# Two transformer blocks on one core: the first two jobs take x without its norm, x arrives in column blocks, and ada blocks change places

## The reference

```python
def rmsnorm(x, g):
    xf = x.astype(jnp.float32)
    y = xf * lax.rsqrt(jnp.mean(jnp.square(xf), axis=-1, keepdims=True) + NORM_EPS)
    return (y * g.astype(jnp.float32)).astype(x.dtype)
...
        h = rmsnorm(x, g[0])
        proj = h @ w_in[l]
        (u_pool, u_conv, c_gate, b_gate_conv, q, k, v, qi, ki, wi) = jnp.split(proj, pts, axis=-1)
...
        dots = jnp.einsum('bthd,bsd->bths', qib.astype(jnp.float32), k_idx32)
        score = jnp.einsum('bth,bths->bts', wb.astype(jnp.float32) * IDX_HEADS ** -0.5,
                           jax.nn.relu(dots))
...
        shift, scale, gate = jnp.split(silu_c @ w_ada[l] + b_ada[l], 3, axis=-1)
```

## Time and profile before

| what | value |
|---|---|
| median of three runs | 2193.26 us (2193.22 to 2193.27) |
| the profiled execution's own time | 2193.32 us |
| its span, first to last instruction | 2191.5 us |
| mean granted TensorE clock | 0.999 |
| TensorE busy | 2180.9 us, 15930 products |
| VectorE busy | 1546.1 us, 71% |
| ScalarE busy | 1060.4 us, 48% |
| GpSimd busy | 103.1 us |
| DMA | 474.97 MB, mean 217 GB/s |

### The profile page before, as it was taken

How to read it: one execution, slowest core, us unless ns; L and a number is a source line. 1 busy time by engine, 2 the same in 40 slices (tenths; PEclk the granted TensorE clock), 3 DMA queues, 4 the chain that set the end, 5 groups by cost and what they waited for, 6 DMA issues and landing times.

```text
span 2191.5 us, 37576 instructions
## 1 busy us (share of the span) xinstructions
PE 2180.9 (100%) x15930; PEld 2050.2 (94%) x15930; DVE 1546.1 (71%) x1886; ACT 1060.4 (48%) x1382; POOL 103.1 (5%) x84
## 2 busy tenths in 40 slices
PE   9999999999999999999999999999999999999998
PEld 9999999999999889989988988998889999999987
DVE  7899588888889657544554555555768887776776
ACT  5444445544444546444543443444655555444443
POOL 1000000000000000000000000000101211110001
PEclk9999999999999999999999999999999999999999
DMA  8876676687787755656656656656755545678784
GB/s 276 245 242 199 199 252 223 227 279 259 253 282 263 240 183 182 194 192 193 195 194 194 194 194 196 200 191 204 246 172 164 165 136 178 220 269 285 257 276 158
DMA packets 248032, 474.97 MB, mean 217 GB/s; under 512 B 21526, under 2 KB 26000, under 8 KB 247096
## 3 DMA queue, kind: packets, MB, share of 16 engines
q1 hardware_dynamic: 243032, 454.40, 64.9%
q0 software_dynamic: 4832, 18.16, 2.5%
HBM read 468.30 MB, written 5.78 MB: 216 GB/s over the span
## 4 chain that ended last, share of the span: by engine, by line
PE 98%; DVE 1%; issue 0%; ACT 0%; DMA 0%; SPq 0%; DVEq 0%; POOLq 0%; POOL 0%; ACTq 0%
PE ps L907 21%; PE ps L909 20%; PE ps L908 20%; PE ps L900 11%; PE ps L901 11%; PE ps L902 11%; PE ps L825 1%; PE ps L703 0%; PE ps L748 0%; DMA raw<-in_w_in 0%; PE ps L735 0%; PE ps L814 0%; PE ps L813 0%; PE ps L815 0%; DVE wloW L1298 0%
## 5 line engine op out<-in xcount | busy, mean ns | idle before, releaser
L907 PE MATMUL ps<-op0h,whiW 128*128 128x256 f32 x3376 | 936.9, 278 | 1.4 <-DVE wloW L1298 1.2
L909 PE MATMUL ps<-op0h,wloW 128*128 128x256 f32 x3376 | 932.3, 276 | 0.0
L908 PE MATMUL ps<-op0l,whiW 128*128 128x256 f32 x3376 | 932.2, 276 | 0.0
L1298 DVE TENSOR_TENSOR wloW<-raw,whiW 128x1024 fp32r<-128x1024 f32 (+1 forms) x503 | 618.2, 1241 | 312.3 <-ACT whiW L954 310.3
L954 ACT ACTIVATE whiW<-raw 128x1024 fp32r<-128x1024 f32 (+1 forms) x504 | 529.7, 1059 | 574.6 <-PE ps L909 469.2
L907 PEld LDWEIGHTS ps<-op0h,whiW 128*128 128x128 f32 x3376 | 633.8, 188 | 4.0 <-DVE wloW L1298 2.1
L908 PEld LDWEIGHTS ps<-op0l,whiW 128*128 128x128 f32 x3376 | 633.9, 188 | 0.6
L909 PEld LDWEIGHTS ps<-op0h,wloW 128*128 128x128 f32 x3376 | 633.8, 188 | 0.0
L1298 DVE TENSOR_TENSOR wloT<-raw,whiT 128x1024 fp32r<-128x1024 f32 (+1 forms) x264 | 318.9, 1218 | 236.2 <-ACT whiT L954 235.0
L954 ACT ACTIVATE whiT<-raw 128x1024 fp32r<-128x1024 f32 (+1 forms) x264 | 273.9, 1048 | 286.2 <-PE ps L902 246.4
L900 PE MATMUL ps<-whiT,op1h 128*128 128x512 f32 x640 | 249.2, 389 | 0.0
(11 more groups left out here) (310 smaller groups left out, 2088.4 us busy)
## 6 DMA issues: line engine op xcount, KB each, us to landing
raw<-in_w_in SPq DMA_DIRECT2D x256, 512.0 KB, 4.3
raw<-in_w_up SPq DMA_DIRECT2D x128, 512.0 KB, 3.8
raw<-in_w_down SPq DMA_DIRECT2D x128, 512.0 KB, 4.0
raw<-in_w_ada SPq DMA_DIRECT2D x96, 512.0 KB, 4.5
raw<-in_w_gate SPq DMA_DIRECT2D x96, 512.0 KB, 5.0
raw<-in_w_out SPq DMA_DIRECT2D x64, 512.0 KB, 4.8
raw<-in_w_branch SPq DMA_DIRECT2D x48, 512.0 KB, 5.0
raw<-in_w_proj_a SPq DMA_DIRECT2D x24, 512.0 KB, 5.0
```

Source lines behind the costliest of these rows:

```text
L907: pe.matmul(o, wh, xh[:, ka, :], start=first and m % 2 == 0, stop=False, skip_group_check=True)
L908: pe.matmul(o, wh, xl[:, ka, :], start=False, stop=False, skip_group_check=True)
L909: mm = pe.matmul(o, wl, xh[:, ka, :], start=False, stop=last, skip_group_check=True)
L1298: v.tensor_tensor(wlo[job.mode][q % NSPL][:, :, 0:job.n], x, h.bitcast(F32), ALU.subtract).then_inc(s_lo, 1)
```

## The change

- x is issued by ScalarE's queue in four blocks of 512 columns (both halves of the tokens), the norm gains behind the first; SyncE's queue begins with ident and the weights, and the gate's vectors come behind raw buffer 3.
- The first operand is x turned and scaled by the gain alone: ScalarE writes it to x0t, VectorE splits it (split_x0: a copy that rounds, and a subtraction). qi0 and qi1 take it so. The missing factor rstd goes into wi, which is scaled by it in vw's epilogue.
- The row sums move to steps 8 and 9, rstd behind them; x0_diagonal puts rstd on the diagonal of two 128x128 tiles, and one product with a matrix of ones spreads it over all partitions (256 columns). For pairs p = 0 to 7, at steps 12, 13, 14, 16, 17, 18, 20, 21, VectorE multiplies x0t by it (x0_norm), ScalarE rounds (x0_high) and, in the next step, VectorE subtracts (x0_low). kk's chunk p waits for pair p.
- The warm-ups are 7, 2 and 2 in place of 12, 4, 1 and 1.
- The load of pw waits for the eighth pair; vectors_b gets a transpose of 48 columns, and its sigmoid moves from step 6 to 23.
- ada blocks 0 to 12 stood behind chunks 10, 13, 16, 19, 22 and 32 to 53 in threes; they now stand behind 32 to 53 in threes (blocks 0 to 7) and 64, 69, 74, 79, 84. The quarters of blocks 0 to 7 move with them, from steps 36 and 37 to 51 and 52.

```diff
-        for q in (list(range(of["qi1"].first + 2, of["vw"].first, 3)) + list(range(of["pool0"].first, NQ, 3)))[:13] + list(range(of["q0"].first + 2, NQ, 3))[:51]:
+        for q in (list(range(of["pool0"].first, of["cc0"].first, 3)) + list(range(of["cb0"].first, of["q0"].first, 5)))[:13] + list(range(of["q0"].first + 2, NQ, 3))[:51]:
...
-        side(act_at, 6, "vectors_b")
-        side(dve_at, 7, "vectors_b", 1)
+        side(act_at, 23, "vectors_b")
+        side(dve_at, 24, "vectors_b", 1)
+        for tt in range(2):
+            side(act_at, 8 + tt, "x0_square", tt)
+            side(dve_at, 8 + tt, "x0_var", tt)
+        side(dve_at, 10, "x0_diagonal")
+        side(pe_at, 11, "x0_spread")
+        side(dve_at, 11, "x0_spread")
+        for p, q in enumerate((12, 13, 14, 16, 17, 18, 20, 21)):
+            side(dve_at, q, "x0_norm", p)
+            side(act_at, q, "x0_high", p)
+            side(dve_at, q + 1, "x0_low", p)
...
-            for t in range(2):
-                sp.dma_start(x0[:, t, :], rows_of("x", t)).then_inc(s_x[t], 16)
             sp.dma_start(ident[:, :], a["k_ident"]).then_inc(s_ident, 16)
-            sp.dma_start(vst[0:64, :], a["norm_gains"].rearrange("l g (r c) -> (l g r) c", c=128)).then_inc(s_va, 16)
-            sp.dma_start(vst[64:112, :], a["b_gate"].rearrange("l g (r c) -> (l g r) c", c=128)).then_inc(s_va, 16)
...
-            rstd("x0", 0)
-            rstd("x0", 1)
...
+            rstd("x0", 0)
+            rstd("x0", 1)
+            pool.wait_ge(s_xnop, 8)
+            pool.dma_start(pw[:, :, :, :], a["pool_w"].rearrange("l g (c p) d -> p (l g) c d", p=128)).then_inc(s_pw, 16)
...
+                pe.wait_ge(s_x[u // 2], 16)
+                if u >= 3:
+                    pe.wait_ge(s_x0s, 2 if u < 5 else u - 2)
+                for j in range(2):
+                    turn_x0_part(2 * u + j, turned_x0(u, j))
...
+            def x0_spread():
+                pe.wait_ge(s_ones, 1)
+                pe.wait_ge(s_diag, 1)
+                pe.wait_ge(s_oper, 8)
+                pe.matmul(bank[6][:, 0:256], ones, diagonal, start=True, stop=True).then_inc(s_spread, 1)
...
+                elif job.name == "kk":
+                    pe.wait_ge(s_xnop, k // 2 + 1)
...
-            warm(12)
+            warm(7)
             pe.wait_ge(s_ident, 16)
-            pe.wait_ge(s_va, 32)
-            pe.transpose(bank[7][:, 0:112], vst[0:112, :], ident[0:112, 0:112]).then_inc(s_vst, 1)
-            warm(4)
+            pe.wait_ge(s_va, 16)
+            pe.transpose(bank[2][:, 0:64], vst[0:64, :], ident[0:64, 0:64]).then_inc(s_vst, 1)
             turn_x(0)
-            warm(1)
+            warm(2)
             turn_x(1)
-            warm(1)
+            warm(2)
...
+            columns_of_x(0)
+            act.dma_start(vst[0:64, :], a["norm_gains"].rearrange("l g (r c) -> (l g r) c", c=128)).then_inc(s_va, 16)
+            for j in range(1, 4):
+                columns_of_x(j)
...
+            def x0_high(p):
+                act.wait_ge(s_pe, of["qi1"].first + p + 1)
+                act.wait_ge(s_xn, p + 1)
+                act.activation(op0h[:, 2 * p:2 * p + 2, :], x0t[:, 2 * p:2 * p + 2, :], ACT.Copy).then_inc(s_xnhi, 1)
...
+            act.activation(col("table"), tmp[0][:, 0:2], ACT.Identity).then_inc(s_table, 1)
+            act.wait_ge(s_vat, 1)
+            turn_x0_part(0, 0).then_inc(s_x0s, 1)
+            high_first(0)
+            turn_x0_part(0, 1).then_inc(s_x0s, 1)
+            high_first(1)
+            for i in range(1, 3):
+                turn_x(i)
...
+            def split_x0(u, j, n):
+                k = slice(2 * u + j, 2 * u + j + n)
+                v.wait_ge(s_x0s, u + j + 1 if u == 0 else u + 2)
+                v.tensor_copy(op0h[:, k, :], x0t[:, k, :]).then_inc(s_x0hi, 1)
+                v.wait_ge(s_x0hi, u + j + 1 if u == 0 else u + 2)
+                return v.tensor_tensor(op0l[:, k, :], x0t[:, k, :], op0h[:, k, :].bitcast(F32), ALU.subtract)
...
+            def x0_diagonal():
+                v.wait_ge(s_rstd, 2)
+                for tt in range(2):
+                    op = v.tensor_scalar(diagonal[:, 128 * tt:128 * tt + 128], ident[:, :], norm_col("x0", tt)[1], None, ALU.mult)
+                op.then_inc(s_diag, 1)
+            def x0_spread():
+                v.wait_ge(s_spread, 1)
+                v.tensor_copy(spread, bank[6][:, 0:256]).then_inc(s_rb, 1)
+                v.wait_ge(s_rb, 1)
+            def x0_norm(p):
+                x = x0t[:, 2 * p:2 * p + 2, :]
+                v.tensor_tensor(x, x, spread.unsqueeze(1).broadcast_to([128, 2, 256]), ALU.mult).then_inc(s_xn, 1)
+            def x0_low(p):
+                k = slice(2 * p, 2 * p + 2)
+                v.wait_ge(s_xnhi, p + 1)
+                v.tensor_tensor(op0l[:, k, :], x0t[:, k, :], op0h[:, k, :].bitcast(F32), ALU.subtract).then_inc(s_xnop, 1)
...
-                    v.tensor_scalar(wi[:, tt, :], b[:, 256:272], 0.25, None, ALU.mult).then_inc(s_pair[job.pair], 1)
+                    v.tensor_scalar(wi[:, tt, :], b[:, 256:272], norm_col("x0", tt)[1], 0.25, ALU.mult, ALU.mult).then_inc(s_pair[job.pair], 1)
...
+            split_x0(0, 0, 1).then_inc(s_oper0, 1)
             low_first(0)
-            x0_norm(1, 256, 512)
-            low_x0(0, 0)
...
-            low_x0(0, 1)
-            low(1)
-            turn_x(1)
-            low(2)
-            turn_x(2)
-            x0_norm(0, 1024, 2048)
-            x0_norm(1, 1024, 2048)
+            for i in range(1, 3):
+                turn_x(i)
+                low(i)
```

More of the change, by code:

```diff
@@ L329, in program @@
         a5 = tmp[5]
+        spread, diagonal, ones = tmp[4][:, 0:256], tmp[4][:, 256:512], tmp[5][:, 128:256]
         gqk = sb("gqk", [128, 2, 128])
@@ L432, in program @@
         s_const = sem("pool_constants")
-        s_x = [sem(f"x_rows{i}") for i in range(2)]
-        s_va, s_vb, s_ident = sem("vectors_a"), sem("vectors_b"), sem("ident")
+        s_x = [sem(f"x_columns{i}") for i in range(4)]
+        s_va, s_vg, s_vb, s_ident = sem("vectors_a"), sem("gate_vectors"), sem("vectors_b"), sem("ident")
         s_vst, s_vat, s_vsu, s_vbt, s_csig, s_csil = sem("va_turned"), sem("vat"), sem("vb_turned"), sem("vbt"), sem("c_sigmoid"), sem("c_silu")
@@ L704, in turn_x @@
                 mm.then_inc(s_turn, 1)
+            def x0_spread():
[3 more added lines that the diff above has]
+                pe.matmul(bank[6][:, 0:256], ones, diagonal, start=True, stop=True).then_inc(s_spread, 1)
             def vectors_b():
+                pe.wait_ge(s_vg, 16)
+                pe.transpose(bank[3][:, 256:304], vst[64:112, :], ident[64:112, 64:112])
                 pe.wait_ge(s_vb, 128)
@@ L847, in fourier_d @@
                 mm.then_inc(s_fd, 1)
-            parts = {"turn_x": turn_x, "vectors_b": vectors_b, "bias_row": bias_row, "ada_fold": ada_fold, "index_dots": index_dots, "pool_weight": pool_weight,
+            parts = {"turn_x": turn_x, "x0_spread": x0_spread, "vectors_b": vectors_b, "bias_row": bias_row, "ada_fold": ada_fold, "index_dots": index_dots, "pool_weight": pool_weight,
                      "scores1": scores1, "turn1": turn1, "values1": values1, "turn_x": turn_x,
@@ L971, in x2_square, with turn_x0_part @@
                 square(X, macc[:, tt, :], "x2", tt)
+            def turn_x0_part(u, j):
+                kt = 2 * u + j
+                act.wait_ge(s_turn0, 2 * u + 2 if u else kt + 1)
+                return act.activation(x0t[:, kt, :], turned_x0(u, j), ACT.Identity, scale=vat[:, kt:kt + 1])
             def turn_x0(u):
-                for kt in (2 * u, 2 * u + 1):
-                    act.wait_ge(s_turn0, kt + 1)
-                    act.activation(op0h[:, kt, :], bank[4 + kt % 4][:, 0:256], ACT.Identity, scale=vat[:, kt:kt + 1]).then_inc(s_x0hi, 1)
+                turn_x0_part(u, 0)
+                turn_x0_part(u, 1).then_inc(s_x0s, 1)
             def turn_x(u):
@@ L1366, in turn_x, with x0_var @@
                 v.tensor_tensor(l, x, h.bitcast(F32), ALU.subtract).then_inc(s_oper, 1)
+            def x0_var(tt):
+                part, (ss, rs), x = col("x0_parts")[:, tt:tt + 1], norm_col("x0", tt), x0[:, tt, 1024:2048]
+                for j in (2, 3):
+                    v.wait_ge(s_x[j], 16)
+                v.tensor_tensor_reduce(junk0[:, 1024:2048], x, x, 1.0, D * EPS, ALU.mult, ALU.add, ss).then_inc(own.sem, own.up())
+                v.wait_ge(own.sem, own.n)
+                v.wait_ge(s_sumsq, tt + 1)
+                v.tensor_scalar(rs, part, ss, 1.0 / D, ALU.add, ALU.mult).then_inc(s_var, 1)
+            def x0_diagonal():
+                v.wait_ge(s_rstd, 2)
+                for tt in range(2):
+                    op = v.tensor_scalar(diagonal[:, 128 * tt:128 * tt + 128], ident[:, :], norm_col("x0", tt)[1], None, ALU.mult)
[11 more added lines that the diff above has]
+                v.tensor_tensor(op0l[:, k, :], x0t[:, k, :], op0h[:, k, :].bitcast(F32), ALU.subtract).then_inc(s_xnop, 1)
```

97 lines of the change are left out of this document (36 added, 61 removed).

## The result

| | before | after |
|---|---|---|
| median of the runs | 2193.27 us (6 runs, 2193.20 to 2193.96) | 2204.98 us (6 runs, 2204.53 to 2206.07) |
| ratio | 1 | 1.0053, 95% interval 1.0043 to 1.0064 |
| profiled execution: own time, span | 2193.32, 2191.5 us | 2205.14, 2203.3 us |
| busy TensorE, VectorE, ScalarE | 2180.9, 1546.1, 1060.4 us | 2182.9, 1555.6, 1061.8 us |

The change makes the kernel 11.7 us slower; 7.15 us was forecast. The direction held, the range did not: 2205.0 lies 0.5 us above its upper end, 2204.5.

The account below looks back on a forecast made before the run. TensorE was taken as the bound (98% of the span), so only its time without products could change: -4.2 + 0.3 + 0.75 + 5.3 + 5.0 = +7.15 on 2193.3 gives 2200.4 us, range 2196.5 to 2204.5.

Parts of the forecast that it names:

- the start, up to the end of chunk 0: Ahead of TensorE's first product: it comes at 8.9 us, after fewer warm-ups and smaller first loads; -4.2 us.
- chunks 1 and 2: Behind the first chunk: the weight split now follows the turn of the pair, 3.7 us against 3.6; +0.3 us.
- the 48-column transpose, chunk 5: TensorE's own new work: one transpose of 48 columns adds 0.05 us.
- the diagonal's product: TensorE's own new work: one float32 product of 256 columns spreading rstd over all partitions; 0.7 us.
- the norm during qi1 and kk: TensorE waits ahead of chunks 20 to 23 for VectorE and ScalarE to norm eight pairs; +5.3 us.
- the ada blocks and quarters: Ahead of low(70), VectorE has no gap for added blocks 8, 9 and two quarters; TensorE waits, +5.0 us.
- The data must be there by then: At the start: x and w's 1 MB, ident and gains land near 5.8 us, operands are ready at 8.5.
- rival of the late loads: At the start: loads on two queues share, first product near 12 us, about 2202.5 us in all; chance 0.05.
- The ping-pong: In qi1 and kk: VectorE and ScalarE alternate in order, 3.63 us per pair against TensorE's 2.04; +5.3 us.
- The clock: Rival: clock falls in TensorE's pauses ahead of chunks 20-23 and 65-70, costing 1.7 to 3.4 us; chance 0.15.

Follow-up runs that it names:

- e13: e8 with x, gains and weights all loaded on SyncE's queue in the order of need; 2191.51 us (10 runs), ratio to before 0.9991.
- e6: The changed kernel with four of GpSimd's loads (cm, gqk twice, recip) moved behind the store of the bias row; 2203.70 us.
- e7: The changed kernel with the gains' load ahead of x's first block and GpSimd's four loads later; 2203.15 us.
- e8: The changed kernel with five ada blocks and two quarters later, x0_norm one step earlier, gains first, GpSimd's four loads later; 2191.47 us, ratio to before 0.9992.
- e12: The kernel before with x loaded in four blocks of 512 columns instead of two token halves, still on SyncE's queue; 2199.56 us.
- e3: The changed kernel with fourteen extra products of ident with itself on TensorE ahead of chunk 67; 2204.61 us.
- e1: The changed kernel with five ada blocks behind chunks 74, 77, 80, 83, 86 and two quarters at steps 69 and 70; 2199.71 us.
- e5: The changed kernel with the norm gains' load ahead of x's first block on ScalarE's queue; 2206.06 us.
- e9: The changed kernel with fold_map (two reductions of ident and a copy on VectorE) at step 27 instead of 20; 2205.10 us.
- e4: The changed kernel with each x0_norm one step earlier than its x0_high; 2198.31 us.
- e2: The kernel before with the change's ada places and nothing else of the change; 2198.28 us.
- e14: e7 with nine extra products of ident with itself on TensorE ahead of chunk 22; 2203.34 us.

## Why the prediction was wrong

Its terms against what the changed kernel's trace shows, by the chunk times:

| step | forecast | measured |
|---|---|---|
| the start, up to the end of chunk 0 | -4.2 | -2.90 |
| chunks 1 and 2 | +0.3 | +0.36 |
| chunk 3's weights | 0 | +1.23 |
| the 48-column transpose, chunk 5 | +0.05 | +0.33 |
| the diagonal's product | +0.7 | +0.46 |
| the norm during qi1 and kk | +5.3 | +6.20 |
| the ada blocks and quarters | +5.0 | +5.08 |
| behind 800 us | 0 | +1.06 |
| sum | +7.15 | +11.81 |

**The start was the step that failed**, by 2.9 us (-0.98 for -3.85). The sentence that broke is "The data must be there by then", with its 5.8 us: the gains landed at 7.25 us, the first product came 1.1 us late, and -4.2 became -2.9 (0.2 us of that is the sum's own: it set 8.9 against 13.15, where the first product before stood at 12.95). The working put 1 MB and the small loads at 2.6 us per MB, as if they came first and alone. The pace was low, 259 GB/s from 3 to 5 us, where the rows of before ran at 406, but that is the small part: by 5.8 us the changed kernel had moved 1.07 MB, nearly the 1.15 MB that the working counts. The gains were not among them. They stood on ScalarE's queue, the second row below, while SyncE's went on with weights that were wanted later (MB and share of the engines, 4 to 7 us):

```profile
q1 hardware_dynamic: 410, 0.81, 72.9%
q10 hardware_dynamic: 212, 0.27, 30.8%
```

In e13, with one queue in the order of need, the gains landed at 5.70 us, although that kernel had moved less by then (0.86 MB by 5.8 us). From issue to landing they took 6.0 us in the changed kernel and 4.1 in e13:

```profile
vst<-in_norm_gains ACTq DMA_DIRECT2D x1, 32.0 KB, 6.0
vst<-in_norm_gains SPq DMA_DIRECT2D x1, 32.0 KB, 4.1
```

And I followed the loads only up to the first product. The sum has no term for the wait for weights at chunk 3, 1.23 us, behind x's last blocks and GpSimd's loads; they landed at 17.9 us, against 14.2 before. e6 gives the whole of it back by moving four of GpSimd's loads. The +0.3 of chunks 1 and 2 held (+0.36, also in e7 and e8).

That was my rival of the late loads (2202.5 us, chance 0.05). Its mechanism was right, and its reason, queues that share, holds for the gains and for chunk 3; what it left out is the slow pace of x's blocks, which e12 has on one queue as well. By the Trainium skill (DMA: Bandwidth & Descriptors, Issuing engines are not separate DMA queues), transfers of all issuers run on the same 16 engines and interleave. The two queue rows above agree. For the kernel's time the number of queues made no difference, 2191.51 us in e13 against 2191.47 in e8. With 0.05 this rival had far too small a chance, for a stage in which no row showed the loads of the new shape.

The start has luck in it too. The forecast let the warm-ups end at 6.1 us, from the one profile of before, in which the rows change from 0.44 to 0.22 us near 4.75. In profiles with the very same start the fourteen rows took 4.69 us (e3), 4.77 (the change) and 6.30 (e1, whose row is this):

```profile
1.18 6.30 PE L945 MATMUL ps<-tmp 128*128 128x256 f32 x14 [1.18 <-DVE tmp L1933]
```

With the gains at 7.25 us that hardly mattered. Had they landed at 5.8, a profile like e1's would have started near 7.5 all the same, as e5, e8 and e13 do, where the warm-ups end last.

**The ping-pong was right in mechanism, and its term 0.9 us too small.** The steps themselves held: 3.66 us for 3.63, 31.8 us from the first norm to the last subtraction (48.66 to 79.76 + 0.68) for 31.5. What was added is the head, 2.56 us for 2.38, since low(14) waited 0.36 us for ScalarE (47.51 us); 0.25 us by which the diagonal's product was cheaper, so that TensorE arrived sooner; the rest, some 0.2 us, is left by subtraction, perhaps TensorE's own resumption behind the last wait; no run shows it. It is not fold_map (e9), and not the clock, which is 1.00 in this stage of the changed kernel. e4 removes the delay whole, and shows that it was order and not work.

**The ada blocks were right** in place, size (5.08 for 5.0) and reason: e2 gives the same alone, and e1 takes it away. The prediction said 3.2 us by chunk 67 and had waits in pieces; e2 has 3.26 there. In the changed kernel it was 4.67 us, since the clock fell behind the pause, and 5.08 by chunk 70 all the same.

**The clock.** I gave its fall 0.15 and 1.7 to 3.4 us. It fell in the second stretch and cost nothing there (e3). It cost 0.7 us in kk in e7 (e14), and about 0.45 in e5 and e6. Their longest pause there, 2.27 to 2.28 us, is that of the changed kernel, whose clock stayed at 1.00.

**Left open** is the 1.06 us behind 800 us: 0.28 at chunk 293 and 0.82 at chunk 692. At chunk 692 TensorE waits for a weight split behind a late load. At chunk 293 no load is late: VectorE ends the split of that chunk's weights at 841.90 us, behind a row that waited for GpSimd, and TensorE starts on it at 842.04. This first delay, 0.2 to 0.3 us, appears in every form of the changed kernel that is 5.8 us or more late by then, in none that is 5.0 us or less late, and not in e12, which is 6.1 us late. The second is 0.2 to 0.4 us in e1, e4, e5, e6, e9 and e12, and absent in the others, with no order that I can see. It wasn't tried further. Without this 1.06 us the kernel would have taken 2203.9 us, inside the range, with the start just as wrong: the total would then have held by luck.
